# Ends of the layers: three tiles multiplied together while the output weights arrive, and the turned rows brought to one tile behind

## The reference, cut to what matters

```python
# layer 0 (o: gated attention output)   y = o @ attn_w_out + attn_b_out
# layer 1 (o: gated recurrence output)  y = o @ rec_w_out
x = x + rmsnorm(y, post_norm_w[layer])      # layers 0 and 1
h = rmsnorm(x, pre_norm_w[layer + 1])       # input of the next layer
# layer 2
x = x + merged @ w_out
out = rmsnorm(x, final_norm_w)
```

## Time and profile before

| what | value |
|---|---|
| median of 3 runs | 4359.21 us (4358.42 to 4364.45) |
| profiled execution | 4357.68 us, span 4356.4 us |
| PE busy | 3862.5 us, 89% of the span |
| DVE, ACT, POOL busy | 47%, 35%, 21% |
| ends A, B, C in the span | about 771 to 998, 2208 to 2441, 4146 to 4356 us |

### The profile page before, as it was taken

One profiled execution on the slowest core, in us unless ns is written; L12 is line 12 of the kernel. 1 busy time (PEld: TensorE's weight loads), 2 busy tenths in 40 slices (PEclk: granted clock), 3 DMA queues, 4 the chain that ended last, 5 costly groups with the idle time before them and its releaser, 6 DMA issues.

```text
span 4356.4 us, 72842 instructions
## 1 busy us (share of the span) xinstructions
PE 3862.5 (89%) x30496; PEld 2877.9 (66%) x30496; DVE 2064.3 (47%) x4533; ACT 1523.7 (35%) x2905; POOL 928.7 (21%) x814
## 2 busy tenths in 40 slices
PE   7999979896999999999979788888888878999979
PEld 4555558685777777777768566666666664555567
DVE  4665542454555555555544455555565551122222
ACT  2444431223444444444433333333334321222132
POOL 0000011223444433444333221212111100000032
PEclk9999989998999999999989899999999988999989
DMA  3000000221010101010023311111111121010032
GB/s 117 20 1 1 1 20 20 107 87 60 20 39 20 39 20 34 25 35 25 20 87 139 101 36 31 36 31 36 31 31 36 36 79 33 0 29 0 0 111 87
DMA packets 186548, 183.35 MB, mean 42 GB/s; under 512 B 6496, under 2 KB 158320, under 8 KB 186224
## 3 DMA queue, kind: packets, MB, share of 16 engines
q1 hardware_dynamic: 186224, 178.69, 13.0%
HBM read 145.12 MB, written 33.55 MB: 41 GB/s over the span
## 4 chain that ended last, share of the span: by engine, by line
PE 76%; DVE 10%; ACT 7%; issue 4%; DMA 2%; POOL 1%; SPq 0%; DVEq 0%; ACTq 0%; POOLq 0%
PE bank L193 14%; PE bank L195 13%; PE bank L194 13%; PE bank L1598 6%; PE bank L1169 4%; PE bank L447 4%; ACT arena L187 3%; PE bank L1655 3%; PE bank L2071 2%; ACT L277 2%; DVE arena L685 1%; PE bank L2082 1%; DVE arena L178 1%; DVE oT L2487 1%; PE bank L1698 1%
## 5 line engine op out<-in xcount | busy, mean ns | idle before, releaser
L194 PE MATMUL bank<-hT_cut,arena_cut 128*128 128x512 f32 x1824 | 732.5, 402 | 0.0
L187 ACT ACTIVATE arena<-bank 128x512 f32<-128x512 f32 (+1 forms) x584 | 312.9, 569 | 969.7 <-PE bank L195 448.1
L187 ACT ACTIVATE arena<-arena 128x512 f32<-128x512 f32 (+3 forms) x690 | 359.4, 549 | 284.3 <-POOL arena L1352 221.4
L193 PE MATMUL bank<-hT_cut,arena_cut 128*128 128x512 f32 x920 | 432.7, 470 | 8.9 <-DVE hT_cut L1409 8.9
L194 PEld LDWEIGHTS bank<-hT_cut,arena_cut 128*128 128x128 f32 x1824 | 356.1, 195 | 68.8 <-issue 14.9
L188 ACT ACTIVATE arena<-arena 128x256 f32<-128x256 f32 (+2 forms) x336 | 210.1, 626 | 511.3 <-DVE arena L177 276.5
L195 PE MATMUL bank<-hT_cut,arena_cut 128*128 128x512 f32 x920 | 372.9, 405 | 0.0
L193 PE MATMUL bank<-arena_cut,hT_cut 128*128 128x512 f32 x768 | 308.5, 402 | 62.5 <-POOL oT_cut L949 62.5
L193 PE MATMUL bank<-oT_cut,arena_cut 128*128 128x512 f32 x648 | 289.5, 447 | 42.0 <-DVE hT_cut L1409 21.3
L194 PE MATMUL bank<-arena_cut,hT_cut 128*128 128x512 f32 x768 | 305.6, 398 | 0.0
L195 PE MATMUL bank<-arena_cut,oT_cut 128*128 128x512 f32 x768 | 305.4, 398 | 0.0
(11 more groups left out here) (222 smaller groups left out, 7336.2 us busy)
## 6 DMA issues: line engine op xcount, KB each, us to landing
arena<-in_w_in SPq DMA_DIRECT2D x72, 512.0 KB, 3.9
arena<-in_rec_w_in SPq DMA_DIRECT2D x64, 512.0 KB, 4.1
x_after<-arena SPq DMA_DIRECT2D x32, 512.0 KB, 2.6
arena<-x_after SPq DMA_DIRECT2D x32, 512.0 KB, 4.1
oT<-in_x SPq DMA_DIRECT2D x16, 512.0 KB, 3.6
arena<-in_x SPq DMA_DIRECT2D x16, 512.0 KB, 3.6
h_after<-hT SPq DMA_DIRECT2D x4, 2048.0 KB, 7.7
hT<-h_after SPq DMA_DIRECT2D x4, 2048.0 KB, 16.6
```

The lines of the kernel that those rows point to most:

```text
L187: return e.activation(out, a, f, bias=bias, scale=scale)
L193: pe.matmul(out, a[0], b[0], start=start, stop=False)
L194: pe.matmul(out, a[0], b[1], start=False, stop=False)
```

## The change

Three things change, all in `finish_layer`:

1. The ring of banks is split: six banks for m0 and m1 (three tiles), two for turned halves.
2. A step `begin` stands in each queue. ACT and POOL have `cut(0), cut(1), cut(2)` ahead of the weights. PE takes tiles 0, 1 and 2 together: for each weight block c, as soon as its rest is there, it does the 18 matmuls of that block for the six halves. The six halves are complete only with the last block.
3. The order after it is `first(3), rest(0), first(4), rest(1), rest(2), first(5), rest(3), rest(4), first(6), rest(5), first(7), rest(6), ... first(15), rest(14), rest(15)`. SP's queue holds the same DMAs in the same order as before.

```diff
-    banks = Banks(k.bank)
+    banks, hbanks = Banks(k.bank[0:6]), Banks(k.bank[6:8])
...
-    def in_turn(cut, first, rest):
-        cut(0)
-        cut(1)
-        for t in range(NT):
+    AT_ONCE = 3
+
+    def in_turn(cut, begin, first, rest):
+
+        for t in range(AT_ONCE):
+            cut(t)
+        begin()
+        cut(AT_ONCE)
+        cut(AT_ONCE + 1)
+        done = 0
+        for t in range(AT_ONCE, NT):
             if t + 2 < NT:
                 cut(t + 2)
             first(t)
-            if t:
-                rest(t - 1)
-        rest(NT - 1)
+            while done < {3: 1, 4: 3}.get(t, t):
+                rest(done)
+                done += 1
+        for t in range(done, NT):
+            rest(t)
...
     def on_pe():
+        def begin():
+            held = [[banks.take(f"m{n}", t)[0] for n in range(2)] for t in range(AT_ONCE)]
+            for c in range(KC):
+                pe.wait_ge(*w_v.by("lo", c))
+                for t in range(AT_ONCE):
+                    if c == 0:
+                        pe.wait_ge(*c_p.by("lo", t))
+                    for n in range(2):
+                        ins = product(pe, held[t][n], (part(k.hT_cut, t)[:, c, :], part(k.oT_cut, t)[:, c, :]),
+                                      (wo_hi[:, c, n * 512:(n + 1) * 512], wo_lo[:, c, n * 512:(n + 1) * 512]),
+                                      start=(c == 0), stop=(c == KC - 1))
+                        if c == KC - 1:
+                            ins.then_inc(*m_pe.did(f"m{n}"))
...
-                    turn_rows(k, N, banks, junk, t, half, taken)
-
-        in_turn(nothing, first, rest)
+                    turn_rows(k, N, hbanks, junk, t, half, taken)
+
+        in_turn(nothing, begin, first, rest)
...
-        for c in range(KC):
-            a.wait_ge(*w_got[c].by("in"))
-            act(a, wo_hi[:, c, :], wo[:, c, :], ACT.Copy).then_inc(*w_a.did("hi"))
-        in_turn(cut, nothing, rest)
+        def begin():
+            for c in range(KC):
+                a.wait_ge(*w_got[c].by("in"))
+                act(a, wo_hi[:, c, :], wo[:, c, :], ACT.Copy).then_inc(*w_a.did("hi"))
+
+        in_turn(cut, begin, nothing, rest)
```

More of the change, by code:

```diff
@@ L863, in in_turn, with nothing, load_x @@
             first(t)
-            if t:
-                rest(t - 1)
-        rest(NT - 1)
-    def nothing(t):
+            while done < {3: 1, 4: 3}.get(t, t):
[3 more added lines that the diff above has]
+            rest(t)
+    def nothing(t=None):
         pass
     def on_sp():
-        def first(t):
+        def load_x(t):
             if t >= 2:
@@ L877, in first @@
             sp.dma_start(x_at[t % 2], x_in[t * P:(t + 1) * P, :]).then_inc(*x_got[t % 2].did("in"))
+        def begin():
+            load_x(0)
+            load_x(1)
         def rest(t):
@@ L889, in rest @@
                 sp.dma_start(h_out[:, :, g * G:(g + 1) * G], k.hT[:, :, g * G:(g + 1) * G]).then_inc(*h_kept[g].did("in"))
+            if t + 2 < NT:
+                load_x(t + 2)
         for c in range(KC):
@@ L894, in on_sp @@
             sp.dma_start(at, src.unsqueeze(0).broadcast_to([P, D])).then_inc(*r_got.did("in"))
-        in_turn(nothing, first, rest)
+        in_turn(nothing, begin, nothing, rest)
     def on_pe():
+        def begin():
[11 more added lines that the diff above has]
+                            ins.then_inc(*m_pe.did(f"m{n}"))
         def first(t):
@@ L905, in first @@
                 for c in range(KC):
-                    if t == 0 and n == 0:
-                        pe.wait_ge(*w_v.by("lo", c))
                     ins = product(pe, b, (part(k.hT_cut, t)[:, c, :], part(k.oT_cut, t)[:, c, :]),
@@ L960, in rest @@
             root(t, 1)
-        in_turn(cut, nothing, rest)
+        in_turn(cut, nothing, nothing, rest)
     def on_dve():
@@ L998, in rest @@
             for half in range(2):
-                keep_rows(k, N, banks, nw, t, half)
+                keep_rows(k, N, hbanks, nw, t, half)
         for c in range(KC):
@@ L1007, in on_dve @@
         v.wait_ge(*r_got.end())
-        in_turn(nothing, nothing, rest)
+        in_turn(nothing, nothing, nothing, rest)
     on_sp()
```

## The result

The changed kernel takes 4376.32 us (median of 5 runs, 4372.47 to 4379.14) against 4359.21 us: ratio 1.0037, 95% interval 1.0023 to 1.0051. It is slower by 17.1 us where 10 was forecast; sign and mechanism were right, the size was short by 7 us. The measured time is inside the stated range of 8 in 10 (4362 to 4377), but close to its edge, and outside the forecast's own range (4365 to 4374). The profiled execution took 4379.14 us, the longest of the five, so I compare it stretch by stretch.

What follows compares the result with a forecast made beforehand. PE, busy 89% of the span, bounds the kernel, with idle time at the layer ends. -32.4 + 34.0 + 7.7 + 1.7 = +11.0 us on 4357.68 gave 4368.7, forecast 4369 us; own range 4365 to 4374, 8 in 10: 4362 to 4377.

Steps and rivals of the forecast that it cites:

- Starts: Starts of the three layer ends: PE begins 10.3, 10.9 and 11.2 us earlier, together -32.4 us.
- rival 2: Starts of the ends: DVE or POOL alone keeps the shared SBUF port; 4389 us (DVE, 7%) or 4376 us (POOL, 8%).
- Catching up: Two ends that turn rows: PE waits two more whole chains in each, 2 x 9.5 + 2 x 7.5 = +34.0 us.
- Rival 4: Catch-up waits: they cost less than a whole chain, as tile 2's vector work runs ahead of tile 1's turning; 4361 us, 10%.
- The bank: First end: first(4) waits once for tile 1's banks, which DVE empties only behind keep_rows(0); +1.7 us.
- SP: DMA queue: same DMAs in the same order, a near load of x in the second end; 0, at most 2 us.
- Clock behind the waits: Behind the four catch-up waits: transposes and first products run at clock 0.50, 1.9 us each; +7.7 us, bounds 6 and 9.
- The starts' clock: Starts of the three ends: PE's slowness at first stays as it was; 0 us.
- Base: Whole kernel: sum added to the profiled 4357.68 us; the median of the runs lies 1.5 us higher, which gives 4370.2.
- Rival 1: All seven restarts: PE's clock stays at full after idle of 8 to 10 us; 4356 us, not slower, 8%.
- Rival 3: Behind the catch-ups: turned rows (transposes) do not raise the clock, so products run slow 2.0 us longer; 4372 us, 15%.

Runs made afterwards that it cites:

- the fill: Changed kernel with 32 or 24 throw-away matmuls for PE inside each of the four catch-up waits: 4365.23 us, ratio to before 1.0007.

## Why the prediction came out as it did

**Starts (-32.4).** Right: 7.24, 7.28 and 7.23 us from SP's first DMA to PE's first product, so 10.3, 10.9 and 11.2 us earlier, and the cuts put back cost 31.4 us. DVE and POOL took turns, as forecast, and neither kept the other out; rival 2 is out. One half of it had 4376 us, the time that was measured; that is a coincidence, since its mechanism would have had PE start 2.3 us later in each end.

**Catching up (+34.0).** Right to 0.1 us: 28.5 - 9.5 = 19.0 in A, 22.4 - 7.5 = 14.9 in B. The last turned rows of before were a measured sample of the new situation. Rival 4 is out: no wait for L177 was under a chain. Two further runs show what I had only argued, that the price goes with the lag: two tiles cost half, and a lag kept to the end has the same waits.

**The bank (+1.7).** Right: 1.6, once (1.9 with the restart); twelve times when the lag is kept.

**SP (0).** Right: no wait of PE in B is longer than the 7.5 us of before.

**Clock behind the waits (+7.7).** This term was mis-sized: it is 9.2 us in the profiled ends with the fill, 11.1 by the medians. The form was right (1.1 us on eight slow transposes and the rest on products); the length of the slow stretch was not. I took 3.7 us, the mean of the three starts of before (4.5, 2.9, 3.8 us). Seven us from each restart of the changed kernel, first its three starts, then its four catch-ups:

```profile
781.80:788.80 7.00, 7.00 (x20) 5.55 (x21) 7.00 (x5) 5.90 (x7) 1.98 (x1) 0.64 1.02 390
2236.76:2243.76 7.00, 7.00 (x22) 5.58 (x23) 7.00 (x5) 5.90 (x7) 1.94 (x1) 0.71 0.98 393
4188.14:4195.14 7.00, 7.00 (x20) 5.58 (x21) 7.00 (x5) 5.90 (x6) 1.98 (x1) 0.63 1.03 410
853.41:860.41 7.00, 7.00 (x24) 5.92 (x25) 3.80 (x6) 1.15 (x2) 2.71 (x2) 0.64 0.26 75
878.42:885.42 7.00, 7.00 (x27) 5.91 (x28) 3.81 (x6) 1.15 (x2) 2.71 (x2) 0.72 0.27 78
2304.09:2311.09 7.00, 7.00 (x25) 5.92 (x26) 4.04 (x5) 1.76 (x4) 2.71 (x2) 0.64 0.23 77
2327.05:2334.05 7.00, 7.00 (x23) 5.87 (x24) 4.05 (x5) 1.77 (x4) 2.71 (x2) 0.57 0.64 237
```

The slow stretches are 5.0, 4.1 and 5.2 us at the starts and 5.0, 3.9, 5.0 and 6.0 us at the catch-ups. Of these last 19.9 us, 4 x 1.97 are transposes and 12.0 us products, which lose 12.0 x (0.43 - 0.233) / 0.43 = 5.5 us; with 4 x 1.1 us on the transposes that is 9.9 us. I had put 1.7 us of slow products at each place, and it was 3.0 in the mean. The chain of waits in B gives the same loss in another way, by the turnings of tiles 2, 3, 4 and 5:

```profile
2304.09 1.97 PE bank L311 x8
...
2318.70 0.89 PE bank L311 x8
...
2327.05 1.97 PE bank L311 x8
2342.09 0.87 PE bank L311 x8
```

From tile 2's to tile 3's are 14.61 us; less 1.97 of transposes and 11.2 of products at full clock, 1.4 us were lost on products. From tile 4's to tile 5's are 15.04, 1.9 us lost. I had put 0.8 us. My upper bound of 9 for the whole term was a little too low as well. The catch-ups were not a special case: their stretches are as long as those of the starts of the same execution, and the three starts that I had read were a short sample. The second profile of before has 4.3, 6.0 and 4.8 us at the same places.

**The starts' clock (0).** I left it as it was. The starts of the changed kernel ran slow for 14.3 us together, those of the first profile of before for 11.2: 3.1 us more, 1.4 us of time. The second profile of before has 15.1 us, so the change need not be the cause; it is the same scatter.

With these terms the ends close. A: -10.3 + 19.0 + 1.9 + 4.5 (clock behind two waits) + 0.2 (clock at the start) = 15.3, measured 15.5. B: -10.9 + 14.9 + 5.4 + 0.6 = 10.0, measured 10.2. C: -11.2 + 0.6 = -10.6, as measured.

**Base (+1.5 only).** The time is 7.6 us above the 4368.7 that the sum gave. The ends account for 15.1 - 11.0 = 4.1 of them. Another 1.5 is the distance from the profiled execution to the median, which I had named and left out of the forecast. The last 2.0 (17.1 between the medians less 15.1 in the ends) is scatter: the first profile of before was fortunate in phases outside the change, by 5.7 us against a second one, and its median of 4359.21 lies 2.2 us below that of 26 later runs.

Rival 1 (clock stays up) is out: 0.50 behind every wait. Rival 3 had 4372 us, nearer than my 4369, for a wrong reason. By it the slow stretch begins anew behind the transposes, so a catch-up would be slow for 2.0 us longer than a start. The ten catch-ups that stand ahead of products in three kernels (the changed one, the one with late cuts and the one with two tiles) were slow for 3.9 to 6.0 us, 5.0 in the mean and the transposes counted in; thirty starts in ten profiles were slow for 2.9 to 6.1 us, 4.7 in the mean. And with the clock up, 68 transposes held it there.

## What to carry to other kernels

Where each tile ends in a serial chain on other engines and PE must take part in every chain, a lag of n tiles is n - 1 chains that run beside no product, wherever it is worked off. That was seen with one, two and three tiles, with whole tiles of products between the turnings and a chain (8.6 us) that fills most of a tile's 11.2 us of products; a finer interleaving was not tried. Start the products early with one tile and keep the chains one behind; the depth of the opening buys nothing once PE has work from the first block on. And read the price of a new wait from the tail of the old kernel, where the pipeline drains in the same way; add the slow clock behind it, with a slow stretch read from more than one execution: three starts of one profile gave 3.7 us here, thirty of ten profiles 4.7.

## What the runs showed that I had not expected

- The slow stretch behind an idle time of 7.5 to 21.5 us is not of one length: 2.9 to 6.1 us over the starts and catch-ups of ten profiles. At the same place of the same kernel (the start of B, before) it was 2.9 us in one execution and 6.0 in another, which alone moved the end by 1.4 of its 1.7 us.
- Putting throw-away work into four waits gave back 9 to 11 us, most of what the change lost, though no wait became shorter in what it waits for.
- An untouched phase of 1708 us scatters by 6 us between executions, more than some of the terms of this sum; comparing stretch by stretch told 15.1 us of change from 6.3 us of scatter in one profile.
